# Experts with 4 KB weight rows, gate and up as three fp32r products, filled slots alone gathered and scattered to token rows

## The chip, the cores and the metric

The kernel runs on one core of a Trainium2 chip, as one program in one launch. The metric is the device time of the launch in microseconds (us), as the median over runs. A core has five instruction streams that wait for each other through semaphores: TensorE (PE, with its weight loads as PEld), VectorE (DVE), ScalarE (ACT), GpSimd (POOL) and SyncE (SP), which here only issues transfers. DMA engines, sixteen of them, move the data.

## The reference

One encoder layer is applied to 512 and to 1024 tokens with the same weights, 1536 tokens of 1024 features in all. Cut to what matters:

```python
h = h + parallel_mixer(rmsnorm(h, g_mix), ...)
h = h + memory_cross_attention(rmsnorm(h, g_xattn), rmsnorm(mem, g_mem), w_xq, w_xkv, w_xo)
h = h + hierarchical_moe(rmsnorm(h, g_moe), w_router_group, w_router_expert, w_exp_gate, w_exp_up, w_exp_down)
return rmsnorm(h, g_final)

def hierarchical_moe(hn, w_rg, w_re, w_gate, w_up, w_down):
    # top 1 of 4 groups, then the top 2 of its 8 experts; gates[n, e] is their weight, 0 for the other experts
    hg = jnp.einsum('nd,edf->nef', xf, w_gate)          # d 1024, f 128, e 32
    hu = jnp.einsum('nd,edf->nef', xf, w_up)
    act = jax.nn.silu(hg) * hu * gates[..., None]
    out = jnp.einsum('nef,efd->nd', act, w_down)
```

Everything is fp32. Each token has two experts, so 3072 pairs of token and expert have to be computed.

## The kernel before

The program is a list of stages: the mixer with its spatial gating and neighbourhood attention (to about 545 us of the trace), its output product, the memory cross-attention with the norm and logits of the router woven in (to 1043 us), the routing (to 1076 us), the experts (to 1343 us) and the last stage. Tokens are worked on in 12 tiles of 128 (`NT`).

Cross-attention and router. A list `stages`, written out at build time, fixes the order of TensorE's work; `order` is the same list with the norms' steps put between, and ScalarE and VectorE follow it. For the MoE norm, ScalarE squares a tile of `H`, GpSimd computes the reciprocal root (`rsqrt`, L670 to L675, two instructions on one column), VectorE multiplies (the `pre` step, L1206) into one of two buffers `hs`, SP stores that tile to `xn_moe` in HBM (L621), TensorE transposes it, and VectorE copies it out of PSUM times the column `g_moe` (`gain_evac`, L1167) for the logits. SP's queue holds, one behind the other, the loads of the cross-attention's weights, 24 stores of zeros to the result rows of the 24 possible overflow blocks (L614), the stores to `xn_moe`, with the weights of experts 0 and 3 behind the fourth, and the weights of six more experts once all logits are computed.

Routing. VectorE finds group and experts of each token; with TensorE's help every pair gets a slot in a table: 128 slots for each of the 32 experts, and `NOVER` = 24 overflow blocks for what exceeds 128. `slot_src` holds the token of every slot; empty slots hold token 0. `slot` holds the slot of every pair. How many overflow blocks are used is known only on the chip (`over_n`).

Experts. A block is 128 slots of one expert. GpSimd gathers its 128 rows of `xn_moe` with an indirect DMA (L760), two buffers `x_g`. TensorE transposes them, 8 times 128x128 (L1650), and VectorE copies them times `g_moe` to `x_gT` (L1167). With the weights as the stationary and `x_gT` as the moving operand TensorE computes gate and up, 16 fp32 matmuls of 128 columns (L1659); the trace shows each fp32 matmul as two, so 32. ScalarE takes the silu (L996), VectorE the product (L1370), which stands ready as `act_T`; TensorE makes the down product, 2 matmuls of 512 columns (L1666), after the transposes of the next block. ScalarE (L999) and VectorE (L1374) copy one half each to `y_st`, and ScalarE issues a plain store of the 128 rows to `y_exp` (L1002). Weights lie in 8 slots (`RING`); SP refills a slot when the down product of its block is done, by three loads of 512 KB: gate, up (L605, L606) and down (L607). Gate and up are read so that a partition gets 8 pieces of 512 bytes; down gives 4 KB a partition. The 32 blocks of the experts come first, partly in a loop (`expert_blocks`), then a loop over the possible overflow blocks with an `If` around each body.

Last stage. When all stores have landed, GpSimd gathers for each tile the two result rows of every token from `y_exp` (L779), four tiles ahead (`AHEAD`). VectorE adds each to `H` times its gate (L1388, two passes of 1024 columns), ScalarE squares (L1016), GpSimd takes the root, VectorE scales with `gf_row` (L1396), and SP stores. GpSimd issues the gathers of the tile four ahead before a tile's root.

The code uses elsewhere what the change brings to the experts: `split_products` (L418). A number is split in a rounded part, copied by ScalarE to fp32r (`make_hi`, L411), and the difference, by VectorE (`make_lo`, L416), and three fp32r products (L421 to L423) stand for one fp32 product.

## Time and profile before

| | |
|---|---|
| median of 3 runs | 1422.01 us (1419.4 to 1422.91) |
| the profiled execution | 1418.28 us, span 1416.6 us |
| busy: PE, PEld, DVE, ACT, POOL | 1212.8, 953.3, 575.6, 330.8, 193.2 us |
| DMA | 207.17 MB, mean 146 GB/s |
| routing starts (last logits done) | 1043.6 us |
| first gate and up product of the experts | 1084.2 us |
| last result copied out of PSUM | 1343.0 us |
| ScalarE: copy of 128x512 from PSUM (L999), silu of 128x128 (L996) | 597, 277 ns |
| VectorE: product of 128x128 (L1370), copy of 128x512 from PSUM (L1374) | 287, 692 ns |
| GpSimd: the two instructions of a root (L673, L675), median; an issued gather (L760), median | 190, 549, 936 ns |
| ScalarE: square of 128x1024 (L1016), and reading its sum | 1056, 186 ns |

The shares of busy time are averages over stages of very different kinds, so the page is read by stages. In the 40 slices of the page TensorE is near full up to slice 28, drops in the routing, and is empty in the last two slices; the DMA engines are full in the experts. In the rows below, a group of instructions stands with its line, engine, operation, shapes and count; `x` with a number is a count. The granted clock is a share of 2.4 GHz: 1.00 is 2.4 and 0.50 is 1.2 GHz.

### The profile page before, as it was taken

Reading aid. Unit: us, or ns where it says so; the run is one execution under the profiler, and the core shown is the slowest. Engines: PE = TensorE matmul, PEld = TensorE weight load, DVE = VectorE, ACT = ScalarE, POOL = GpSimd, SP = SyncE. Lnnn points to the kernel's source line nnn. Section 1 sums busy time; section 2 is a strip of 40 time slices with the busy share of each in tenths; the row PEclk is TensorE's granted clock in tenths of the full one; section 3 lists DMA queues with packets and bytes.
Section 4 is the critical chain, followed back from the end, with each engine's and each line's share of the span. In section 5 each row is a group of like instructions: output and inputs, shape, how many; then the busy total and the mean of one; then the engine's idle time right before and its main releaser. Section 6 shows DMA issues by size and latency. Waiting matters only on the chain.

```text
span 1416.6 us, 17949 instructions
## 1 busy us (share of the span) xinstructions
PE 1212.8 (86%) x6288; PEld 953.3 (67%) x6288; DVE 575.6 (41%) x1101; ACT 330.8 (23%) x719; POOL 193.2 (14%) x323
## 2 busy tenths in 40 slices
PE   3999999599998995999989989999955999988700
PEld 2888888488877884788844446667745888877600
DVE  4423222421126775333332155344374333333357
ACT  4322222400025553211110143223110111111112
POOL 0221111100012220000010000000001111111075
PEclk9999999899999997999989999999976999999955
DMA  7211111233166115433110930004166999999877
GB/s 232 70 53 59 59 59 30 66 78 73 30 147 176 25 26 178 153 89 89 44 60 0 312 104 0 15 15 134 60 201 194 369 368 370 368 363 358 288 279 254
DMA packets 180730, 207.17 MB, mean 146 GB/s; under 512 B 35775, under 2 KB 140223, under 8 KB 180671
## 3 DMA queue, kind: packets, MB, share of 16 engines
q1 hardware_dynamic: 160462, 139.81, 33.4%
q0 software_dynamic: 10944, 39.85, 7.9%
q10 hardware_dynamic: 9264, 26.74, 5.1%
q8 instruction: 34, 0.56, 0.2%
q14 instruction: 26, 0.21, 0.0%
HBM read 147.34 MB, written 55.10 MB: 143 GB/s over the span
## 4 chain that ended last, share of the span: by engine, by line
PE 65%; SPq 16%; DVE 6%; issue 4%; POOL 3%; DMA 3%; ACT 2%; ACTq 0%; POOLq 0%; DVEq 0%
PE bank L1605 13%; PE bank L421 12%; PE bank L423 12%; PE bank L422 12%; SPq L607 8%; SPq L606 5%; PE bank L1509 3%; PE bank L1489 3%; POOL at L779 2%; PE bank L1498 2%; DVE at L416 1%; PE bank L1444 1%; PE bank L1565 1%; PE bank L1659 1%; SPq L605 1%
## 5 line engine op out<-in xcount | busy, mean ns | idle before, releaser
L421 PE MATMUL bank<-at,at 128*128 128x512 f32 x768 | 310.8, 405 | 28.6 <-DVE at L416 18.7
L423 PE MATMUL bank<-at,at 128*128 128x512 f32 x768 | 303.4, 395 | 0.0
L422 PE MATMUL bank<-at,at 128*128 128x512 f32 x768 | 302.8, 394 | 0.0
L1605 PE MATMUL bank<-at,at 128*128 128x512 f32 (+1 forms) x560 | 186.0, 491 | 5.3 <-DVE at L1167 5.3
L421 PEld LDWEIGHTS bank<-at,at 128*128 128x128 f32 x768 | 147.1, 192 | 59.9 <-DVE at L416 20.3
L1659 PEld LDWEIGHTS bank<-at,at 128*128 128x128 f32 x1248 | 146.0, 194 | 36.7 <-issue 12.8
L423 PEld LDWEIGHTS bank<-at,at 128*128 128x128 f32 x768 | 146.4, 191 | 31.6
L422 PEld LDWEIGHTS bank<-at,at 128*128 128x128 f32 x768 | 147.3, 192 | 29.4
L1659 PE MATMUL bank<-at,at 128*128 128x128 f32 x1248 | 149.0, 279 | 13.4 <-DMA at<-in_w_exp_down 12.0
L1605 PEld LDWEIGHTS bank<-at,at 128*128 128x128 f32 x560 | 93.5, 195 | 90.3 <-issue 85.7
L416 DVE TENSOR_TENSOR at<-at,at 128x1024 fp32r<-128x1024 f32 (+2 forms) x42 | 78.9, 1885 | 138.5 <-ACT at L411 138.5
L673 POOL TENSOR_TENSOR at<-at 128x1 f32<-128x1 f32 x88 | 23.8, 271 | 702.2 <-ACT at L962 330.1
L1167 DVE TENSOR_TENSOR at<-bank,at 128x512 f32<-128x512 f32 x160 | 102.8, 684 | 29.4 <-PE bank L1650 28.4
L411 ACT ACTIVATE at<-at 128x1024 fp32r<-128x1024 f32 (+3 forms) x42 | 66.1, 1582 | 96.6 <-DMA at<-in_w_in 29.8
L1666 PE MATMUL bank<-at,at 128*128 128x512 f32 x156 | 73.4, 593 | 0.0
L760 POOL DMA_INDIRECT at<-xn_moe,at x40 | 37.6, 940 | 250.5 <-PE bank L1650 213.3
L892 ACT ACTIVATE at<-at,at 128x256 f32<-128x256 f32 (+1 forms) x96 | 51.7, 539 | 57.5 <-DVE at L1123 57.3
L1370 DVE TENSOR_TENSOR at<-at,bank 128x128 f32<-128x128 f32 x39 | 11.2, 287 | 130.4 <-PE bank L1659 130.4
L1239 DVE COPY at<-bank 128x512 f32<-128x512 f32 x20 | 13.8, 691 | 121.5 <-PE bank L1605 121.5
L1509 PE MATMUL bank<-at,at 128*128 (+1 forms) x448 | 58.2, 276 | 3.6 <-DMA at<-v_att 3.3
L999 ACT ACTIVATE at<-bank 128x512 f32<-128x512 f32 x39 | 23.3, 597 | 161.6 <-PE bank L1666 161.6
L1489 PE MATMUL bank<-at,at 128*128 (+2 forms) x192 | 57.0, 424 | 3.2 <-POOL at L727 3.2
(158 smaller groups left out, 1250.0 us busy)
## 6 DMA issues: line engine op xcount, KB each, us to landing
at<-in_w_exp_gate SPq DMA_DIRECT2D x39, 512.0 KB, 9.4
at<-in_w_exp_up SPq DMA_DIRECT2D x39, 512.0 KB, 11.1
at<-in_w_exp_down SPq DMA_DIRECT2D x39, 512.0 KB, 11.8
y_exp<-at ACTq DMA_DIRECT2D x39, 512.0 KB, 6.8
y_exp<-at SPq DMA_DIRECT2D x24, 512.0 KB, 7.5
at<-y_mix SPq DMA_DIRECT2D x12, 512.0 KB, 4.5
xn_moe<-at SPq DMA_DIRECT2D x12, 512.0 KB, 2.6
at<-in_w_in SPq DMA_DIRECT2D x2, 2048.0 KB, 12.3
```

Of the source, the lines that this page charges most:

```text
L416: nc.vector.tensor_tensor(lo, x, hi.bitcast(F32), ALU.subtract).then_inc(lo_made, 1)
L421: nc.tensor.matmul(out, w_hi, x_hi, start=(k == 0), stop=False)
L422: nc.tensor.matmul(out, w_lo, x_hi, start=False, stop=False)
L423: last = nc.tensor.matmul(out, w_hi, x_lo, start=False, stop=(k == len(terms) - 1))
L606: sp.dma_start(w_gu[n][:, 1], a["w_exp_up"][0, one].rearrange("e (k p) f -> p (e k) f", p=P)).then_inc(w_e_here[n], 16)
L607: sp.dma_start(w_dn[n], a["w_exp_down"][0, one].rearrange("e p d -> (e p) d")).then_inc(w_e_here[n], 16)
L1167: nc.vector.tensor_tensor(dst, bank[first_bank + n][:].rearrange("p (k t) -> p k t", k=4), g, ALU.mult).then_inc(done, 1)
L1489: nc.tensor.matmul(bank[2 * (s % 2) + n][:, 0:P * len(keys)], q, k, start=True, stop=True).then_inc(s_done, 1)
L1509: last = nc.tensor.matmul(bank[6 + s % 2][:, n * P:(n + 1) * P], na_pT[s % 2][:, n, k * P:(k + 1) * P], vals[:, 4 * kg + 2 * (s % 2) + n, ...
L1605: mm = nc.tensor.matmul(b if kind == "route" else b[:], w, x, start=(k == 0), stop=(k == len(steps) - 1))
L1659: mm = nc.tensor.matmul(out[:, 0:P], w_gu[n][:, half_gu, k], x_gT[n % 2][:, k], start=(k == 0), stop=(k == KT - 1))
L1666: mm = nc.tensor.matmul(bank[5 + k][:], act_T[n % 2], w_dn[n][:, k * HALF:(k + 1) * HALF], start=True, stop=True)
```

## The change

1. Gate and up weights are read so that a partition gets rows 8p to 8p+7 of a weight matrix, one piece of 4 KB. So k now counts rows within a partition, and `x` has to be in the same order: the MoE norm writes its features in that order (VectorE, with `g_moe` as a row `gm_row` multiplied in), so the gain is applied before the store and no longer when transposed tiles are copied. `gm_row` is loaded behind the last query product, at the place of a part of `h_T`, and no tile of the MoE norm is scaled before.
2. Empty slots get a token number that is out of bounds and are skipped by the gathers; the six gather buffers are cleared once, so that skipped rows hold finite numbers. Results are scattered by an indirect DMA of GpSimd to `y_tok`, row k x 1536 + token for the k-th expert of a token; `y_exp`, the zero fills and the issue by ScalarE go.
3. For the 32 experts gate and up are 24 fp32r products with x as the stationary operand and the 256 columns of gate and up as the moving one. x and weights are split by ScalarE and VectorE. The activations now come out with tokens on the partitions, so TensorE transposes them (one 128x128) and ScalarE copies them. Overflow blocks keep fp32 products, with x stationary too.
4. The down product of block b-1 stands behind gate and up of block b. There are 6 weight slots instead of 8; gate and up of a slot are refilled when its gate and up products are done, down when its down product is done. 6 gather buffers instead of 2. The blocks of the 32 experts are written out, with no loop.
5. Last stage: SP loads the two rows of each token from `y_tok` with plain loads, 6 tiles ahead. ScalarE multiplies the first with its gate, GpSimd adds `H`, VectorE adds the second times its gate.

The core of the diff:

```diff
-RING = 8
-AHEAD = 4
+RING = 6
+AHEAD = 6
@@ SP
-            sp.wait_ge(fill_made, 3)
-            for b in range(NE, NBLK):
-                sp.dma_start(y_exp[b * P:(b + 1) * P]..., zeros...).then_inc(unused_filled, 16)
+            sp.wait_ge(mm_done, n_groups["q", NCH - 1, XH - 1] + 1)
+            sp.dma_start(gm_row, a["g_moe"][0].partition_broadcast(P)).then_inc(consts_here, 16)
...
+                sp.dma_start(w_gu[n][:, 0], a["w_exp_gate"][0, one].rearrange("e (p k) f -> p (e k) f", p=P)).then_inc(w_e_here[n], 16)
...
+            for e in range(RING, NE):
+                sp.wait_ge(gu_done, e - RING + 1)
+                load_gate_up(e, e % RING)
+                sp.wait_ge(y_done, e - RING + 1)
+                load_down(e, e % RING)
...
+            sp.wait_ge(y_sent[0], 16 * (NE // 2) + 16 * ((used + 1) // 2))
+            sp.wait_ge(y_sent[1], 16 * (NE // 2) + 16 * (used // 2))
+                for k in range(2):
+                    sp.dma_start(y_g[t][k], y_tok[k * T + t * P:k * T + (t + 1) * P]).then_inc(yg_here[t % AHEAD], 16)
@@ GpSimd
+            for j in range(RING):
+                pool.memset(x_g[j], 0.0).then_inc(zeroed, 1)
...
+            for b in range(NE):
+                pool.wait_ge(xgt_done, 2 * (b + 1))
+                gather(b + RING)
+                scatter(b)      # waits for y_evac_s, y_evac_v of b
...
+            def add_first(t):
+                pool.wait_ge(f_gated, t + 1)
+                pool.tensor_tensor(y_g[t][0], y_g[t][0], H[:, t], ALU.add).then_inc(f_first, 1)
@@ ScalarE, a block
+                    split_xg(b + 1)
+                    split_expert(b + 1)
+                silu(b, b % 2)
+                if b >= 1:
+                    evac_y(b - 1, (b - 1) % 2, (b - 1) // 2)
+                evac_act(b, b % 2)
@@ ScalarE, last stage
+                nc.scalar.activation(y_g[t][0], y_g[t][0], ACT.Copy, scale=gate[:, 0, t:t + 1]).then_inc(f_gated, 1)
@@ VectorE
+                        dve.wait_ge(consts_here, 16 * 8)
+                        nc.vector.scalar_tensor_tensor(hs[n % 2]..., H[:, t]..., r, gm_row..., ALU.mult, ALU.mult).then_inc(n_ready, 1)
...
+                    split_xg(b + 1)
+                    split_expert(b + 1, 0)
+                gated(b, b % 2)
+                if b + 1 < NE:
+                    split_expert(b + 1, 1)
+                if b >= 1:
+                    evac_y(b - 1, (b - 1) % 2, (b - 1) // 2)
...
+                nc.vector.scalar_tensor_tensor(H[:, t], y_g[t][1], gate[:, 1, t:t + 1], y_g[t][0], ALU.mult, ALU.add).then_inc(f_add, 1)
@@ TensorE
+                split_products(bank[2 + j][:, 0:2 * FE].rearrange("p (h f) -> p h f", h=2),
+                               [(x_gT_hi[j][:, k], x_gT_lo[j][:, k], w_gu_hi[j][:, :, k], w_gu_lo[b % RING][:, :, k])
+                                for k in range(KT)]).then_inc(gu_done, 1)
...
+            for b in range(NE):
+                transpose_xg(b + 1, (b + 1) % RING, (b + 1) // RING)
+                gate_up(b)
+                if b >= 1:
+                    down(b - 1, (b - 1) % 2, (b - 1) % RING)
+                transpose_act(b, b % 2)
+            down(NE - 1, (NE - 1) % 2, (NE - 1) % RING)
+            def overflow(b, j, n, r, half):
+                gate_up_whole(b, j, n, r)
+                transpose_xg(b + 1, (n + 1) % RING, r + (n + 1) // RING)
+                transpose_act(b, j)
+                down(b, j, n)
```

## Rows read from the trace of the kernel before

**Rows 1.** Stretches: us, busy (count) PE, PEld, DVE, ACT, POOL; clock, DMA, GB/s.

```profile
1100.00:1250.00 150.00, 149.25 (x1069) 125.54 (x1068) 54.43 (x96) 21.26 (x49) 22.47 (x24) 1.00 1.08 368
...
1350.00:1380.00 30.00, 0.00 (x0) 0.00 (x0) 18.30 (x15) 5.86 (x11) 24.84 (x25) 0.50 0.90 314
```

**Rows 2.** DMA issues: tensors, queue, count, KB each, median us to landing.

```profile
at<-in_w_exp_gate SPq DMA_DIRECT2D x39, 512.0 KB, 9.4
...
at<-in_g_final SPq DMA_DIRECT2D x1, 512.0 KB, 4.0
```

**Rows 3.** The chain of waits from 1000 us: start us, us, what.

```profile
1080.89 1.96 PE bank L1650 x8
...
1084.21 5.93 PE bank L1659 x32
...
1098.89 3.57 PE bank L1659 x32
...
1102.47 0.87 PE bank L1650 x8
...
1103.34 1.73 PE bank L1666 x4
...
1203.08 4.44 SPq L607
...
1410.10 1.28 DVE at L1396
```

**Rows 4.** VectorE in order of time: start us, us, what [idle before].

```profile
1342.35 0.69 DVE L1374 COPY at<-bank 128x512 f32<-128x512 f32 x1 [0.54 <-PE bank L1666]
...
1357.18 2.60 DVE L1388 SCALAR_TENSOR_TENSOR at<-at,at,at 128x1024 f32<-128x1024 f32 x2 [14.15 <-DMA at<-y_exp,at]
...
1387.18 1.28 DVE L1396 SCALAR_TENSOR_TENSOR at<-at,at,at 128x1024 f32<-128x1024 f32 x1 [0.72 <-POOL at L675]
...
1391.70 1.29 DVE L1396 SCALAR_TENSOR_TENSOR at<-at,at,at 128x1024 f32<-128x1024 f32 x1 [0.72 <-POOL at L675]
```

**Rows 5.** Stretches inside w_xkv's load and inside loads of experts.

```profile
562.00:564.00 2.00, 0.00 (x0) 0.00 (x0) 1.97 (x3) 0.00 (x0) 0.00 (x0) 0.50 1.03 424
...
1062.00:1064.00 2.00, 0.00 (x0) 0.00 (x0) 1.79 (x7) 0.00 (x0) 0.00 (x0) 0.50 1.16 322
```

**Rows 6.** TensorE in order of time: fp32r of 512 and of 56 columns.

```profile
130.11 0.39 PE L423 MATMUL bank<-at,at 128*128 128x512 f32 x1
...
130.34 0.39 PE L421 MATMUL bank<-at,at 128*128 128x512 f32 x1
...
1073.12 2.76 PE L1640 MATMUL bank<-at,at 128*128 128x56 f32 x12 [2.70 <-DVE at L1352]
```

**Rows 7.** Groups by form, VectorE and ScalarE: xcount | busy us, mean ns | idle.

```profile
L1167 DVE TENSOR_TENSOR at<-bank,at 128x512 f32<-128x512 f32 x160 | 102.8, 684 | 29.4 <-PE bank L1650 28.4 <-PE bank L1565 0.8
...
L416 DVE TENSOR_TENSOR at<-at,at 128x1024 fp32r<-128x1024 f32 x32 | 39.2, 1225 | 111.3 <-ACT at L411 111.3
...
L1206 DVE TENSOR_SCALAR at<-at,at 128x1024 f32<-128x1024 f32 x28 | 20.8, 747 | 2.5 <-POOL at L675 2.5
...
L411 ACT ACTIVATE at<-at 128x1024 fp32r<-128x1024 f32 x24 | 25.2, 1052 | 48.5 <-DMA at<-in_w_in 24.6 <-DVE at L1034 12.9 <-DVE at L1167 11.0
```

**Rows 8.** The gathers of the experts (L760): from issue to landing.

```profile
DMA to landing us min/median/max: 4.2/7.2/8.8
```

**Rows 9.** VectorE and GpSimd at 270 us, in order of time.

```profile
269.72 4.13 DVE L1084 TENSOR_SCALAR at<-at,at 128x512 f32<-128x512 f32 x1 [1.68 <-POOL at L675]
...
269.64 3.94 POOL L709 MEMSET at<- 128x4608 f32 x1
```

**Rows 10.** GpSimd in the last stage, in order of time.

```profile
1397.64 1.48 POOL L675 TENSOR_TENSOR at<-at 128x1 f32<-128x1 f32 x1
```

**Rows 11.** Groups by form, GpSimd.

```profile
L727 POOL COPY at<-at 64x256 f32 x36 | 22.7, 631 | 73.0 <-PE bank L1489 71.8
...
L701 POOL TENSOR_SCALAR at<-at 128x1440 f32<-128x1440 f32 x1 | 1.7, 1691 | 0.1
```

359 lines of the change are left out of this document (215 added, 144 removed).

## Prediction

> **What bounds the kernel now.** Read the stretches view first: from 1100 to 1250 us TensorE is busy all but 0.75 us, and so are the DMA engines, at a share of 1.08 and 368 GB/s; from 1350 to 1380 us TensorE is idle, at the lower of its two granted levels (0.50, 1.2 GHz) [rows 1]. So two stages are at stake: the experts (39 blocks: 32, and 7 overflow blocks, by the count of issues [rows 2]) and the last stage. Then the chain of waits. Early in the experts it runs through TensorE alone, 3.57 us of gate and up, 0.87 us of transposes and 1.72 us of down products, 6.16 us a block; later through the sync queue, where an issue of one weight load lasts 4.44 us because the queue is backed up [rows 3]. A block moves three weight tensors of 0.52 MB [rows 2] and 128 rows of 4 KB each way, 2.62 MB, at 368 GB/s 7.1 us. That is over 6.16 us, so the 8 slots loaded ahead run out and the stage ends at the pace of the transfers: first gate-up at 1084.21 [rows 3], last copy of a result at 1342.35 plus 0.7 [rows 4]. In the last stage GpSimd paces: it issues two indirect gathers a tile, and final scalings of successive tiles stand 4.52 us apart (1387.18, 1391.70) [rows 4]. From 1343.05 to the span's end at 1416.6 are 73.55 us.
>
> **Bytes.** Weights stay 1.57 MB a block. Only the 3072 filled slots are now gathered and scattered, 12.6 MB each way, instead of 39 times 128 rows. The stage moves 61.3 + 25.2 = 86.5 MB instead of 102. What of the rate? A load in 4 KB rows ran at 424 GB/s, the expert loads alone, two thirds of them in 512 byte pieces, at 322 [rows 5]. All is 4 KB now; I take 400 to 420 GB/s in the mix (368, today's mix, is the low end). From block 0 to 31 some 50 MB of weights and 22 MB of rows move: 181 us at 400, 196 at 368. Six slots are full when the stage begins and a slot is refilled four blocks before its use, which covers some 13 us. 168 to 183 us is the demand of the transfers; TensorE will want 179 (below). So the transfers stop being the bound, narrowly.
>
> **TensorE per block.** Gate and up change from 32 half-products of 128 columns (3.57 us) to 24 fp32r products (hi·hi, lo·hi, hi·lo for 8 k) of 256 columns. No fp32r product of 256 columns is in the trace. An fp32r product of 512 columns starts 0.227 us after the one before, at the full clock (2.4 GHz); a 128 column half-product of fp32, which the chain gives 3.57/32 = 0.112 us, passes its columns twice, so it does as much array work; an fp32r product of 56 columns takes 2.76/12 = 0.23 us at the lower level, 0.115 at the full one [rows 3, 6]. Those set 0.112 to 0.120 (0.227 less half of the 0.213 that 512 columns take at 2.4 GHz); the far bound is 0.227, the price of 512. I take 0.116: 2.78 us. With transposes 0.87, down 1.72, and the new transpose of the activations 0.11, a block takes 5.48 us, 0.68 less than 6.16. The activations' round (silu, product, and now a transpose and a copy) lies behind the down products of the block before.
>
> **The other engines in a block.** ScalarE: two copies of x at 0.6, two of the weights at 1.05, silu 0.28, the turned activations 0.28, the result 0.6 (0.6 and 0.28 as in the table): 4.5 us. VectorE: two differences of x at 0.69, two of the weights at 1.23, the product 0.29, the result 0.69: 4.8 us [rows 7]. Both are under 5.48 and walked through in their order, each instruction after the one it waits for, no wait of TensorE ends later than its own work: the last difference for block b+1 ends about when the down products of b-1 do, the transposes of b+2 (0.87) ahead of its use. GpSimd now issues a gather and a scatter: 0.94 us each when undisturbed, as in the table. A result buffer is wanted again 2 x 5.48 - 0.7 = 10.3 us after it is full; the scatter takes about 1.2 us to get its descriptors past a VectorE instruction and lands 7.2 us after, as the gathers do [rows 8]. 8.4 against 10.3 us. For what slips in these two narrow places I add 0.1: 5.6 us a block.
>
> **Overflow blocks.** They stay fp32: 16 half-products of 256 columns at 0.215 (half of 1.73/4 [rows 3]) are 3.44 us; their activations' round isn't hidden: 0.9 for silu and product, 0.11, then 0.6 for the copy of x that ScalarE does first, 0.3, 1.72 for down. 6.75 us each, 47 for seven.
>
> **When the stage ends.** The transposes of block 0 began at 1080.89 at the lower level and took 1.96 us; block 0's half-products took 5.93 instead of 3.57, so the level rose among them [rows 3]. One more VectorE step ahead of the table makes the start 1081.2; transposes 2.0, the split 1.5, block 1's transposes 2.0, and 24 products at 2.8 plus the same 2.0 or so for the level: 1091.5. The second block waits for its split weights: 1096.4. 30 x 5.6 gives 1264.4, its rest 4.2, overflow 47.3, last copy 0.9, branches 1.5: 1318.3, without what comes ahead.
>
> **Ahead of the experts.** The gain of the MoE norm moves to a row that is loaded when the last query product is done; a like row landed in 4.0 us [rows 2]. VectorE waits for it in line, with the result of the first output product queued behind it; TensorE has two banks, 3.4 us of products, before it waits as well: +3.1 (0 if later waits absorb it). The norm's product goes from 0.75 [rows 7] to 1.28 us (a pass of that kind [rows 4]); three of them stand in the tail: +1.6. The six clearings of gather buffers on GpSimd (0.9 us each by 3.94 us for 4608 columns [rows 9]) run while VectorE routes: 0 to 5, I take 1. Table step 0.3. Sum +6 (bounds 0 to 11). The 24 zero fills were hidden behind products: 0. So the last copy is at 1324.3, 18.7 us earlier.
>
> **The last stage.** Loads can start when the last scatter has landed: 1.0 to issue, some 4.2 in all (the quickest gather [rows 8]), then the first two loads of a queue of twelve, 4.7: 9.0 after the last copy (the gathers: 14.1, to 1357.18 [rows 4]). Bytes: 1.57 MB a tile, 3.8 us at 410 GB/s. But the work of a tile moves: ScalarE scales (1.06) and squares (1.25), GpSimd adds two 128x1024 tiles, VectorE does two three-operand passes instead of three. GpSimd and VectorE shut each other out: a VectorE product over 512 columns took 4.13 us beside a 3.94 us GpSimd clearing, where 1024 columns take 0.75, and the second instruction of GpSimd's root took 1.48 us instead of 0.55 beside a VectorE pass [rows 9, 10]. If a long GpSimd addition and a VectorE pass with two tile operands do so too, the tile costs their sum. The addition isn't in the trace: a one-operand pass over 1440 elements takes 1.69 us, 1.20 for 1024; a copy of 256 takes 0.63, 2.5 for 1024 [rows 11]. With two operands I take twice the first, 2.3. Sum: 2.3 + 0.19 + 0.55 (the root, as in the table) + 2 x 1.28 = 5.6 us a tile, against 4.52. First sum of rows ready at 9.0 + 1.06 + 2.3 = 12.4; 11 x 5.6 = 61.6; last pass, square, root, scaling 4.7; last store 5.2 (from 1411.4 [rows 3] to 1416.6). 83.9 us against 73.55: +10.3.
>
> The Trainium skill, SBUF — State Buffer, section "SBUF: two separate sides", states that the port pair is held for a whole instruction by either a GpSimd instruction or a VectorE one in a two-port mode, or one with two SBUF inputs when GpSimd reads SBUF. The rows show the first kind and GpSimd's side of the second; that a long GpSimd addition stops VectorE no row shows. By this rule the last stage goes as in my sum; without it as in the first rival. The GPSIMD Engine Reference, section "Performance versus the Vector engine", gives 4497 ns for an addition of 2048 fp32; half of that, an estimate, is 2.25 us and would leave the sum as it is.
>
> **Sum.** -18.7 + 10.3 = -8.4: span 1408.2. The profiled execution took 1418.28, 1.7 over its span; the median of the runs is 1422.01, 3.7 above it. 1422.0 - 8.4 = 1413.6; I say 1413. Its own range, from 1.2 or 2.5 us for the addition, 5.4 to 5.9 us a block and 0 to 11 us ahead: 1399 to 1428.
>
> **Rivals.** (1) The last stage overlaps. GpSimd then needs 3.0 us a tile, VectorE 2.6, and bytes set 3.8: 12.4 + 41.8 + 4.7 + 5.2 = 64.1, 9.5 less than now; with the experts 28.2 less: 1394. For it: two VectorE passes took 2.60 us, as ever, beside GpSimd's issues of gathers [rows 4]. Against: the 4.13 us row. Chance 0.24. (2) Slower: the scatter or the transfers pace the blocks. VectorE's weight differences shut GpSimd out, the scatter lands over 10.3 us after its buffer is full, and the copy of b+2 waits; at 6.3 us a block it costs 0.7 x 32 = 22: 1436. It decides when a landing exceeds some 9 us (8.4 expected); slower than before from 5.9 us a block on. Chance 0.17. (3) The change doesn't do what it says: an fp32r product of 256 columns costs 0.227. Then 24 x 0.111 x 32 = 85 us more, 1498. Against: 128 and 512 columns of fp32 go as their columns. Chance 0.06.
>
> **How the numbers follow.** Forecast 0.53, rivals 0.24, 0.17, 0.06. 0.3% is 4 us, about what a measurement of this kernel tells from no change: 1418 and 1426 are the borders. Of the forecast's 0.53, 0.31 lies under 1418 and 0.11 within; with the first rival faster is 0.55, same 0.12, slower 0.33. 8 in 10 takes in the first rival and most of the second: 1388 to 1438.
>
> **What will show it.** Starts of successive fp32r products 0.116 us apart in a block; blocks 5.5 to 5.7 us apart with TensorE idle for nothing; DMA near 400 GB/s with short sync issues; overflow blocks 6.7 apart; VectorE passes of 1.28 us stretched to 3.5 beside GpSimd additions of 2.3 in the last stage, tiles 5.6 apart. A last stage with tiles under 4.5 us apart, or blocks over 6, makes the prediction wrong.

## The result, and the profile after

The median of the changed kernel is 1427.34 us (1422.74 to 1430.34, 15 runs), that of the kernel before, run beside it, 1421.02 us (1414.3 to 1423.38, 15 runs). The ratio is 1.0042, 95% interval 1.003 to 1.0055: slower, by 6 us, where 1413 and "faster" were forecast. The profiled execution has a span of 1425.7 us, 9.1 above the one before; the profile of before is of an execution that was 2.7 us quicker than its median (1418.28 against 1421.02), that of after is the median itself, so the difference of the spans is some 3 us too large.

Where it went is read by laying four points of time beside each other. All are read from the two traces: the last copy of router logits, the first silu of an expert block, the silu of block 31 (the last of the 32 experts), and the end of the last copy of a result.

| | before | after | difference |
|---|---|---|---|
| last logits copied (start) | 1043.6 | 1062.7 | +19.1 |
| first silu, block 0 | 1088.03 | 1110.86 | +22.8 |
| block 0 to block 31 | 198.6 | 182.4 | -16.2 |
| block 31 to the last copy's end (7 overflow blocks) | 56.4 | 54.3 | -2.1 |
| last copy's end to the end of the span | 73.6 | 78.2 | +4.6 |
| sum of the last four | | | +9.1 |

The experts are shorter, as the change wanted. What is lost is lost ahead of them and behind them.

Ahead of them. The norm's pass by its line after (duration min/median/max in ns, first and last start; the second line is what it waited for, us and times); the pass of before is in [rows 7]:

```profile
L1278 DVE SCALAR_TENSOR_TENSOR at<-at,at,at x12: 2053/2140/2362, 938.9 to 1051.0; 128x1024 f32<-128x1024 f32 x12
...
  DMA at<-in_g_moe: 3.0, 1
```

The new pass takes 2.14 us in the median, against 0.75. The one wait for the gain row is 3.0 us. In the same stretch GpSimd's root of the norm is stretched beside it, and TensorE runs dry (stretches of after; columns as in [rows 1]):

```profile
L687 POOL TENSOR_TENSOR at<-at x10: 189/700/1508, 953.8 to 1049.9; 128x1 f32<-128x1 f32 x10
```

```profile
980.00:990.00 10.00, 6.54 (x39) 5.65 (x38) 4.84 (x7) 3.12 (x6) 1.15 (x2) 0.85 0.80 319
...
1020.00:1030.00 10.00, 6.83 (x39) 5.76 (x38) 4.05 (x5) 1.15 (x2) 1.12 (x2) 0.90 0.14 54
...
1050.00:1060.00 10.00, 9.80 (x53) 9.59 (x53) 5.93 (x9) 0.00 (x0) 3.42 (x14) 0.59 0.26 105
```

TensorE is busy 6.5 and 6.8 us of 10, and the granted clock falls to 0.85, 0.90 and, in the last products of the router, 0.59. Dips of the clock are in the kernel before as well (0.68 from 1010 to 1020 us); what is new is the tail. Here are the 10 us ahead of the last copy of logits, before and after:

```profile
1033.60:1043.60 10.00, 9.60 (x82) 8.90 (x81) 5.78 (x12) 1.15 (x2) 2.49 (x13) 1.00 0.27 107
```

```profile
1052.70:1062.70 10.00, 9.94 (x48) 9.80 (x47) 3.25 (x8) 0.00 (x0) 0.87 (x3) 0.50 0.13 52
```

TensorE is busy in both, at 2.4 GHz before and at 1.2 GHz, the lower of the two levels, after: the tail of the stage is paid at half speed.

In the experts, TensorE in order of time, and then ScalarE's silus of blocks 14 to 16, both after:

```profile
1204.22 0.28 PE L421 MATMUL bank<-at,at 128*128 128x256 f32 x1
1204.34 0.28 PE L422 MATMUL bank<-at,at 128*128 128x256 f32 x1
1204.45 0.28 PE L420 MATMUL bank<-at,at 128*128 128x256 f32 x1
```

```profile
1188.27 0.28 ACT L1039 ACTIVATE at<-bank 128x128 f32<-128x128 f32 x1
1195.20 0.26 ACT L1039 ACTIVATE at<-bank 128x128 f32<-128x128 f32 x1
1202.20 0.26 ACT L1039 ACTIVATE at<-bank 128x128 f32<-128x128 f32 x1
```

An fp32r product of 256 columns starts 0.12 us after the one before (median 0.120; the 24 of a block stand 0.123 apart in the mean). The first 14 gaps between silus are 5.53 us in the mean; those shown, at block 14, are 6.93 and 7.00, and from block 14 to 28 the mean is 6.35. So there are two halves: TensorE paces the first, something else the second. The wait that is named there is ScalarE's, for a load (us in total, times, longest, from 1180 to 1280 us):

```profile
ACT at L410 <- DMA at<-in_w_exp_down: 25.2, 15, 2.5
```

The last stage, VectorE and GpSimd in order of time, one tile:

```profile
1385.50 2.35 POOL L806 TENSOR_TENSOR at<-at,at 128x1024 f32<-128x1024 f32 x1
1385.57 3.37 DVE L1502 SCALAR_TENSOR_TENSOR at<-at,at,at 128x1024 f32<-128x1024 f32 x1 [0.44 <-POOL at L689]
...
1387.82 1.17 POOL L687 TENSOR_TENSOR at<-at 128x1 f32<-128x1 f32 x1
1388.86 1.27 DVE L1494 SCALAR_TENSOR_TENSOR at<-at,at,at 128x1024 f32<-128x1024 f32 x1
1389.06 1.48 POOL L689 TENSOR_TENSOR at<-at 128x1 f32<-128x1 f32 x1
...
1390.57 3.36 DVE L1502 SCALAR_TENSOR_TENSOR at<-at,at,at 128x1024 f32<-128x1024 f32 x1 [0.44 <-POOL at L689]
```

VectorE's final pass is issued 0.07 us after GpSimd's addition of 2.35 us and lasts 3.37 instead of 1.28 [rows 4]: it does its work when the addition has ended. The root's small instructions (1.17, 1.48) last as long as the VectorE passes beside them. Tiles stand 5.00 us apart, against 4.52 [rows 4].

### The profile page after: what moved, and what is told of

Read it like the earlier page. It is cut to its first block, busy times and chain, and to the rows that moved or that the text cites. A ratio compares the mean times of both kernels' runs of the same rounds, so it can differ in the third digit from the quotient of the medians.

```text
span 1425.7 us, 17488 instructions
## 1 busy us (share of the span) xinstructions
PE 1212.4 (85%) x5959; PEld 939.1 (66%) x5959; DVE 664.7 (47%) x1146; ACT 449.6 (32%) x905; POOL 277.5 (19%) x362
## 3 DMA queue, kind: packets, MB, share of 16 engines
q0 software_dynamic: 13824, 31.48, 6.0%
## 4 chain that ended last, share of the span: by engine, by line
PE 74%; DVE 7%; DMA 6%; issue 4%; POOL 3%; ACT 3%; SPq 2%; ACTq 0%; POOLq 0%; DVEq 0%
PE bank L420 14%; PE bank L422 13%; PE bank L421 13%; PE bank L1711 13%; PE bank L1791 3%; PE bank L1615 3%; DMA at<-in_w_exp_down 3%; PE bank L1595 3%; DVE at L415 2%; PE bank L1777 2%; PE bank L1604 2%; PE bank L1757 2%; POOL at L806 1%; PE bank L1550 1%; ACT at L410 1%
## 5 line engine op out<-in xcount | busy, mean ns | idle before, releaser
L420 PE MATMUL bank<-at,at 128*128 128x512 f32 (+1 forms) x1024 | 387.9, 379 | 27.8 <-DVE at L415 17.9
L421 PE MATMUL bank<-at,at 128*128 128x512 f32 (+1 forms) x1024 | 377.4, 369 | 0.0
L422 PE MATMUL bank<-at,at 128*128 128x512 f32 (+1 forms) x1024 | 377.2, 368 | 0.0
L420 PEld LDWEIGHTS bank<-at,at 128*128 128x128 f32 x1024 | 197.4, 193 | 61.7 <-DVE at L415 21.8
L415 DVE TENSOR_TENSOR at<-at,at 128x1024 fp32r<-128x1024 f32 (+2 forms) x106 | 157.0, 1484 | 168.3 <-ACT at L410 155.3
L422 PEld LDWEIGHTS bank<-at,at 128*128 128x128 f32 x1024 | 197.2, 193 | 32.2
L421 PEld LDWEIGHTS bank<-at,at 128*128 128x128 f32 x1024 | 197.6, 193 | 29.5
L1711 PE MATMUL bank<-at,at 128*128 128x512 f32 (+1 forms) x560 | 192.2, 503 | 11.1 <-DVE at L1295 5.8
L687 POOL TENSOR_TENSOR at<-at 128x1 f32<-128x1 f32 x88 | 37.2, 423 | 702.7 <-ACT at L986 336.6
L410 ACT ACTIVATE at<-at 128x1024 fp32r<-128x1024 f32 (+3 forms) x106 | 130.5, 1268 | 119.6 <-DMA at<-in_w_in 29.8
L1711 PEld LDWEIGHTS bank<-at,at 128*128 128x128 f32 x560 | 97.2, 204 | 99.3 <-issue 92.4
L1791 PE MATMUL bank<-at,at 128*128 128x512 f32 x156 | 74.2, 597 | 3.3 <-ACT at L1043 3.3
L1316 DVE COPY at<-bank 128x512 f32<-128x512 f32 x20 | 13.8, 691 | 122.7 <-PE bank L1711 122.7
L986 ACT ACTIVATE at<-at 128x1024 f32<-128x1024 f32 x28 | 29.6, 1056 | 120.0 <-PE bank L1671 112.2
L785 POOL DMA_INDIRECT y_tok<-at,at x39 | 39.9, 1024 | 140.9 <-DVE at L1463 92.1
L778 POOL DMA_INDIRECT at<-xn_moe,at x45 | 58.6, 1301 | 41.9 <-issue 41.2
L689 POOL TENSOR_TENSOR at<-at 128x1 f32<-128x1 f32 x88 | 57.7, 656 | 6.9
L1615 PEld LDWEIGHTS bank<-at,at 128*128 128x128 f32 x448 | 54.6, 194 | 3.3 <-issue 2.9
L1757 PE MATMUL bank<-at,at 128*128 128x128 f32 x320 | 43.3, 280 | 7.5 <-issue 6.0
```

Source lines behind the costliest of these rows:

```text
L410: nc.scalar.activation(hi, x, ACT.Copy).then_inc(hi_made, 1)
L415: nc.vector.tensor_tensor(lo, x, hi.bitcast(F32), ALU.subtract).then_inc(lo_made, 1)
L420: nc.tensor.matmul(out, w_hi, x_hi, start=(k == 0), stop=False)
L421: nc.tensor.matmul(out, w_lo, x_hi, start=False, stop=False)
L422: last = nc.tensor.matmul(out, w_hi, x_lo, start=False, stop=(k == len(terms) - 1))
L689: pool.tensor_tensor(rs[:, col:col + 1], ms_eps[:, col:col + 1], neg_half, ALU.pow).then_inc(out_sem, 1)
```

## The experiments

The theory after the result: the permuted VectorE pass (its two tile operands are read in steps of 32 bytes, its result is written straight) costs what is lost ahead of the experts; in the second half of the experts the weights come too slowly; in the last stage the GpSimd addition shuts VectorE out. Rivals: the norm's later place and the wait for its row; TensorE or the scatter in the experts; the transfers in the last stage.

### The gain row alone, in the kernel before

```diff
+            sp.wait_ge(mm_done, n_groups["q", NCH - 1, XH - 1] + 1)
+            sp.dma_start(gm_row, a["g_moe"][0].partition_broadcast(P)).then_inc(gm_here, 16)
             sp.wait_ge(fill_made, 3)
             for b in range(NE, NBLK):
...
-                    nc.vector.tensor_scalar(hs[n % 2], src, rs[:, 4 + n % 2:5 + n % 2], None, ALU.mult).then_inc(n_ready, 1)
+                        nc.vector.scalar_tensor_tensor(hs[n % 2], H[:, t], r, gm_row, ALU.mult, ALU.mult).then_inc(n_ready, 1)
```

> The kernel before with one part of the change alone: the gain of the MoE norm is loaded as a row once the last query product is done, the norm's VectorE pass becomes a product of three operands with that row, all in straight order, and it may not stand ahead of that point; the evacuations of the transposes drop the gain. Theory (the permuted pass is what costs ahead of the experts): the pass takes 1.28 us instead of 0.75, and the last logits, at 1043.6 before, come 3 to 7 us later, the time is 0.2 to 0.5% above before. Rival (the later place and the wait for the row cost it, whatever the order of the elements): the logits come 15 to 19 us later and the time is 1.0 to 1.4% above before.

1453.04 us (1449.54 to 1454.03, 4 runs), 1.0222 of before (1.0189 to 1.0256); last logits at 1079.2, 35.6 us late. By its numbers neither theory. Its trace from 940 to 1060 us shows what it was (DMA issues there, and what was waited for from 950 us):

```profile
y_exp<-at SPq DMA_DIRECT2D x24, 512.0 KB, 6.9
```

```profile
ACT at L966 <- DMA xn_moe<-at: 25.6, 1, 25.6
```

The 24 zero fills, 12.6 MB, which the kernel before issues from 783 us on and has behind it by then, were held back by the new wait on the sync queue and ran ahead of the stores of the normed rows; ScalarE waited 25.6 us for one such store, whose buffer it wanted. The fault is the experiment's place for the wait, not the row. It is also a lesson on this change: its early wait on SP is cheap only since the fills are gone.

### The same, in permuted order

```diff
-                        nc.vector.scalar_tensor_tensor(hs[n % 2], H[:, t], r, gm_row, ALU.mult, ALU.mult).then_inc(n_ready, 1)
+                        nc.vector.scalar_tensor_tensor(hs[n % 2].rearrange("p (k q) -> p k q", k=KT), H[:, t].rearrange("p (q k) -> p k q", k=KT), r,
+                                                       gm_row.rearrange("p (q k) -> p k q", k=KT), ALU.mult, ALU.mult).then_inc(n_ready, 1)
...
-                sp.dma_start(w_gu[n][:, 0], a["w_exp_gate"][0, one].rearrange("e (k p) f -> p (e k) f", p=P)).then_inc(w_e_here[n], 16)
+                sp.dma_start(w_gu[n][:, 0], a["w_exp_gate"][0, one].rearrange("e (p k) f -> p (e k) f", p=P)).then_inc(w_e_here[n], 16)
```

> The kernel before with the gain row as above, and the pass reads and writes in the permuted order (32 byte steps), with the router and the expert gate and up weights in 4 KB pieces to match; fp32 products, gathers, scatters and the last stage are as before. Theory (the permuted pass costs): each pass 2.1 to 2.4 us, last logits 15 to 19 us after 1043.6. Rival (place): the same as the kernel with the straight row, under 2 us apart. For the experts: if 512 byte pieces held the transfers back (322 GB/s against 424), the stage from the first gate and up to the last copy (258.8 us before) becomes 5 to 13 us shorter, since TensorE at 6.16 us a block bounds it then; if they did not, it stays within 3 us.

1443.9 us (1443.07 to 1447.21, 4 runs), 1.017 (1.0136 to 1.0204). The same fills stand in its way, so its front (logits at 1086.3) says little: 7 us over the straight one. The pass takes 2055/2150/2354 ns; it reads in steps and writes straight, other than the expectation has it. What the run does show: from the first result copy's start to the last 234.3 us, against 249.6 before. The pair is repeated below with the fills out of the way.

### The straight norm in the changed kernel

```diff
-                        nc.vector.scalar_tensor_tensor(hs[n % 2].rearrange("p (k q) -> p k q", k=KT), H[:, t].rearrange("p (q k) -> p k q", k=KT), r,
-                                                       gm_row.rearrange("p (q k) -> p k q", k=KT), ALU.mult, ALU.mult).then_inc(n_ready, 1)
+                        nc.vector.scalar_tensor_tensor(hs[n % 2], H[:, t], r, gm_row, ALU.mult, ALU.mult).then_inc(n_ready, 1)
...
-                    mm = nc.tensor.transpose(bank[k // 4][:, (k % 4) * P:(k % 4 + 1) * P], x_g[n][:, k * P:(k + 1) * P], ident)
+                    mm = nc.tensor.transpose(bank[k // 4][:, (k % 4) * P:(k % 4 + 1) * P], x_g[n].rearrange("p (q k) -> p k q", k=KT)[:, k], ident)
```

The router's weights are loaded in the order that suits.

> The changed kernel with the norm's pass in straight order; the router's weights are loaded to suit, and the expert transposes read the gathered rows in steps of 8 elements, so that the 4 KB weight pieces stay. Theory: the pass takes 1.28 us, the last logits come at 1047 to 1052 instead of 1062.7, all behind it moves by as much, and the time falls by 10 to 15 us, to 0.994 to 0.998 of before. Rival (place and wait): logits at 1060 or later, the time within 3 us of the changed kernel, 1.003 of before. If TensorE's strided reads cost, the transposes of an expert block take over 0.87 us and the blocks stand over 5.7 us apart instead of 5.58.

1415.11 us (1412.0 to 1418.55, 10 runs), 0.996 (0.9943 to 0.9977); the changed kernel has 1.0042. One pass in another order turns slower into faster, by 12 us of the medians. By line:

```profile
L1278 DVE SCALAR_TENSOR_TENSOR at<-at,at,at x12: 1274/1278/1285, 938.8 to 1042.2; 128x1024 f32<-128x1024 f32 x12
...
  DMA at<-in_g_moe: 3.1, 1
  POOL at L689: 0.4, 1
```

```profile
L1311 DVE COPY at<-bank x12: 186/196/196, 956.1 to 1048.8; 128x36 f32<-128x36 f32 x12
```

The last logits come at 1048.8: 13.9 us earlier than with the permuted pass, and 5.2 after the kernel before. The wait for the row is still there (3.1 us), as is the later place; they are not the cause. The twelve passes are 10.7 us shorter together (15.3 against 26.1 us of busy time). The rest hangs on them, and the delay can be followed along the stage: the copies of logits come later in the changed kernel by 3.1 us at the first tile, 2.5 at the third, 5.9 at the fourth, 8.5 at the ninth, and 13.9 at the twelfth. GpSimd's root has a median of 0.191 us again. From 980 to 1050 us the clock is much the same (0.94 here, 0.93 in the changed kernel); in the 10 us ahead of the last copy it is 0.98 here and 0.50 there.

How sure are these differences? Single executions reach this stage up to 4 us apart: eight kernels here that share the straight norm and the same front have their last logits between 1047.5 and 1051.7. Counted from the last norm pass ahead of the MoE norm (at 884.7 us before, 885.8 in the changed kernel) the scatter is gone: 163.0 to 163.3 us to the last logits in all eight and in the kernel before with the straight row behind the fills (below), 176.9 and 176.7 in the two permuted ones, 158.9 before. So the order costs 13.7 us, and row, place and wait together some 4.2.

The step of 32 bytes is now in TensorE's reading of the gathered rows:

```profile
L1756 PEld LDWEIGHTS bank<-at,at x320: 185/193/226, 1087.2 to 1330.2; 128*128 128x128 f32 x160
L1756 PE MATMUL bank<-at,at x320: 272/274/450, 1087.2 to 1330.3; 128*128 128x128 f32 x160
```

The same in the changed kernel, with straight reads:

```profile
L1757 PEld LDWEIGHTS bank<-at,at x320: 137/140/231, 1100.9 to 1343.6; 128*128 128x128 f32 x160
L1757 PE MATMUL bank<-at,at x320: 272/273/448, 1101.0 to 1343.7; 128*128 128x128 f32 x160
```

The gathered rows are what the weight loads of the transposes read, and these take 193 ns instead of 140. They run beside the matmuls of 274 ns, so almost nothing of it is seen in the time: the blocks of the first half stand 5.59 us apart instead of 5.57, and the means of the two halves are those of the changed kernel (5.54 and 6.36 us).

### 512 byte pieces in the changed kernel

The norm straight, and gate and up loaded with "e (k p) f", so that the transposes read straight too.

> The changed kernel with the norm's pass in straight order and the gate and up weights in 512 byte pieces again, so that nothing reads in steps. Up to the experts it does what the kernel above does. If the 4 KB pieces are needed (322 to 368 GB/s with 512 byte pieces), a block of about 2.25 MB takes 6.1 to 7.0 us, the blocks after the slots loaded ahead stand over 6 us apart, and the experts take 12 to 40 us longer than in the kernel above. If the smaller number of bytes alone is enough, the blocks stand 5.6 us apart and both kernels agree within 3 us.

1429.96 us (1425.59 to 1432.86, 8 runs), 1.0066 (1.0045 to 1.0086). Block 0 to 31 takes 194.6 us against 182.7 with 4 KB pieces, +11.9, just under the low end of the first expectation; the medians of the time are 14.9 apart. The first 11 gaps are 5.6 or less, against 14, so what is loaded ahead lasts three blocks less; from block 14 to 28 the mean is 6.87 against 6.36. Stretches from 1180 to 1280 us, first with 512 byte pieces, then with 4 KB (the last two columns are DMA share, which is the mean busy share of the DMA engines, and GB/s):

```profile
1180.00:1280.00 100.00, 88.49 (x551) 68.41 (x550) 64.34 (x89) 59.40 (x104) 29.65 (x29) 0.98 1.04 332
```

```profile
1180.00:1280.00 100.00, 93.46 (x595) 73.57 (x595) 69.98 (x95) 63.51 (x112) 36.47 (x33) 1.00 0.98 365
```

### The last stage's additions on VectorE

```diff
-                pool.wait_ge(f_gated, t + 1)
-                pool.tensor_tensor(y_g[t][0], y_g[t][0], H[:, t], ALU.add).then_inc(f_first, 1)
...
-                nc.vector.scalar_tensor_tensor(H[:, t], y_g[t][1], gate[:, 1, t:t + 1], y_g[t][0], ALU.mult, ALU.add).then_inc(f_add, 1)
+                nc.vector.scalar_tensor_tensor(H[:, t], y_g[t][0], gate[:, 0, t:t + 1], H[:, t], ALU.mult, ALU.add).then_inc(f_first, 1)
+                nc.vector.scalar_tensor_tensor(H[:, t], y_g[t][1], gate[:, 1, t:t + 1], H[:, t], ALU.mult, ALU.add).then_inc(f_add, 1)
```

The norm is straight, and ScalarE's multiplications by the first gate go as well.

> The changed kernel with the norm's pass in straight order, and in the last stage the additions go back to VectorE: three passes a tile in its own order, as before, with the plain loads kept; GpSimd only does the root, ScalarE only the squares. Theory (a GpSimd addition and VectorE's passes shut each other out, so the tile costs their sum, 5.01 us): the tile takes 3 passes of 1.28 us, 3.85 to 4.0 us, and no pass is stretched; from the last result copy to the end 62 to 65 us instead of 78.8; the time is 14 to 16 us below the kernel that differs in the straight norm alone, 1399 to 1401 us. Rival (the transfers of 1.57 MB a tile set it, at the 367 GB/s of the experts): tiles 4.3 us apart, 67 to 69 us from the last copy, 1404 to 1406. If neither the engines nor the transfers but a chain of waits across engines set it, the tile stays near 5 us.

1398.35 us (1397.8 to 1402.84, 5 runs), 0.984 (0.9824 to 0.9856): it beats both kernels. VectorE in the last stage:

```profile
1383.11 1.28 DVE L1494 SCALAR_TENSOR_TENSOR at<-at,at,at 128x1024 f32<-128x1024 f32 x1 [0.44 <-POOL at L689]
...
1384.31 1.28 DVE L1484 SCALAR_TENSOR_TENSOR at<-at,at,at 128x1024 f32<-128x1024 f32 x1
1385.62 1.28 DVE L1486 SCALAR_TENSOR_TENSOR at<-at,at,at 128x1024 f32<-128x1024 f32 x1
1386.83 1.28 DVE L1494 SCALAR_TENSOR_TENSOR at<-at,at,at 128x1024 f32<-128x1024 f32 x1
```

No pass is stretched; the final passes go from 1351.29 to 1393.1, 3.80 us a tile; from the end of the last copy (1336.77) to the end 64.4 us, against 78.85 in the kernel that differs in this alone (1412.9 less 1334.05). The transfers move 402 GB/s from 1345 to 1365 us and 379 from 1365 to 1385, so they are near, but do not set the pace: after the first tile VectorE waits for no load, only for GpSimd's root, 3.4 us in all.

### fp32 products for all blocks

With the straight norm; blocks 0 to 31 use the overflow blocks' gate and up product, and nothing is split:

```diff
-                gate_up(b)
+                gate_up_whole(b, b % 2, b % RING, b // RING)
```

> The changed kernel with the straight norm, and gate and up of all blocks as fp32 products (16 half-products of 256 columns, x stationary) as in the overflow blocks; no splits of weights or rows on ScalarE and VectorE. Theory (in the second half of the experts the transfers pace, 6.2 us a block, and TensorE's gain counts only in the first half at 5.58): the block takes 3.44 + 0.87 + 1.72 + 0.11 = 6.14 us throughout, the experts become 4 to 8 us longer than in the kernel with split products, the time 1419 to 1423. Rival (the transfers are slowed by what ScalarE and VectorE do, or TensorE paces throughout): the same time within 2 us, or 18 us longer (32 x 0.57).

1422.27 us (1418.52 to 1424.12, 10 runs), 1.0007 (0.9993 to 1.0021). The gaps are 6.16 us from the second to the last; block 0 to 31 takes 190.3 us, 7.6 more than with split products. The first 14 gaps are 0.57 longer, the later ones 0.19 shorter. TensorE's 0.6 us a block is worth 7 us, not 19 (32 x 0.6), since in the second half it had been spent waiting. The transfers that hold the split blocks at 6.36 us in the second half do not hold these: at 6.16 from the start, what is loaded ahead is used up so slowly (0.2 us a block) that it lasts for all 32.

### Empty slots gathered too

Two runs on the straight norm: an empty slot reads the last token's row, or, in the second, the row of its own number.

```diff
-            nc.vector.scalar_tensor_tensor(slot_src, bank[2][:, 0:NBLK], float(2 * T), second, ALU.add, ALU.subtract).then_inc(table_ready, 1)
+            step(nc.vector.scalar_tensor_tensor(second, bank[2][:, 0:NBLK], float(2 * T), second, ALU.add, ALU.subtract))
+            nc.vector.tensor_scalar(slot_src, second, float(T - 1), None, ALU.min).then_inc(table_ready, 1)
```

> The changed kernel with the straight norm, and the gathers read a row for every slot, empty ones too (the last token's row), while the scatters still leave them out: 128 rows a gather instead of some 79. Theory (the second half of the experts goes at the transfers' pace, 360 to 380 GB/s): 0.2 MB more a block, so blocks of 6.7 to 6.8 us instead of 6.2 there and the pace is reached earlier: 10 to 17 us longer, 1425 to 1432 us. Rival (the landing of the scatter paces, or TensorE): within 3 us of the kernel that differs in the norm alone, 1415.

1416.94 us (1414.69 to 1419.99, 9 runs), 0.997 (0.9957 to 0.9984): 1.8 us more than without those rows (the intervals overlap), where bytes at a fixed rate gave 10 to 17.

```diff
+            step(nc.vector.tensor_scalar(over_f8, second, float(T), token[1][:, 0:1], ALU.is_ge, ALU.mult))
+            nc.vector.tensor_tensor(slot_src, over_f8, second, ALU.add).then_inc(table_ready, 1)
```

> As the kernel whose gathers read a row for every slot, but an empty slot reads the row of its own number (128 different rows) and not one row over and over. Theory A (leaving empty slots out saves bytes and little time; the weights' own arrival paces): as with the one row, 1415 to 1419 us, experts 0 to 3 us longer than without the empty rows. Theory B (in that run the one row was read cheaply, and bytes count): 6.7 to 6.8 us a block in the second half, 1425 to 1432 us.

1416.58 us (1415.87 to 1417.66, 5 runs), 0.9966 (0.9953 to 0.9979). Block 0 to 31: 184.8 us with different rows, 184.7 with the one row, 182.7 without. So it is not that one row is read cheaply. Here is the same stretch as above, with the spread rows:

```profile
1180.00:1280.00 100.00, 91.04 (x582) 71.79 (x582) 69.38 (x94) 62.26 (x110) 33.49 (x32) 1.00 1.01 394
```

394 GB/s against 365, at nearly the same pace of blocks. The rate is no constant of the stage: with fewer gathered bytes in it, it falls. Leaving the empty slots out of the gathers saves 11 MB (178.9 moved against 189.9) and 2 us. GpSimd's queue has 13824 packets with and without them (42.5 and 31.5 MB): a row that is left out gives up its bytes, not its packet.

### Fewer weight bytes

With the straight norm; from block 6 on the down load of the main blocks fetches 64 of 1024 columns, and the other 960 are weights of an earlier expert, so this kernel's results are not the layer's.

```diff
-                load_down(e, e % RING)
+                sp.dma_start(w_dn[e % RING][:, 0:64], a["w_exp_down"][0, e, :, 0:64]).then_inc(w_e_here[e % RING], 16)
```

> The changed kernel with the straight norm, and from block 6 on only the first 64 of the 1024 columns of the down weights are loaded (that part of the down products then works on older weights), at the same place and with the same waits: 1.08 MB of weights a block instead of 1.57. Theory (the arrival of weight bytes paces the second half of the experts): every one of the 31 gaps between blocks is 5.6 us, the experts become 10 to 12 us shorter than in the kernel with the straight norm alone, 1403 to 1405 us. Rival (the order of release and landing, whatever the bytes: a load is issued so late that its latency shows): gaps over 6 us stay, under 4 us shorter.

1405.77 us (1402.68 to 1408.42, 4 runs), 0.9895 (0.9879 to 0.9911); block 0 to 31 172.6 us, 10.1 less. Silus at the place where the changed kernel's gaps had grown:

```profile
1173.70 0.28 ACT L1039 ACTIVATE at<-bank 128x128 f32<-128x128 f32 x1 [0.23 <-PE bank L422]
1179.28 0.28 ACT L1039 ACTIVATE at<-bank 128x128 f32<-128x128 f32 x1 [0.23 <-PE bank L422]
1184.87 0.28 ACT L1039 ACTIVATE at<-bank 128x128 f32<-128x128 f32 x1 [0.23 <-PE bank L422]
```

5.59 us apart, as are all but the first. So it is the arrival of the weights: scatters, gathers and the order of the waits are unchanged in this run. 12.8 MB of weights less give 10 us, where 11 MB of gathered rows less gave 2.

### The down weights waited for by their own product

Additions on VectorE and the straight norm, and:

```diff
-                act.wait_ge(w_e_here[e % RING], 48 * (e // RING + 1))
+                act.wait_ge(w_e_here[e % RING], 32 * (e // RING + 1))
...
+            def down(b, j, n, r):
+                pe.wait_ge(w_d_here[n], (32 if n == 5 else 16) + 16 * (r + 1))
```

> The kernel with the straight norm and VectorE's additions in the last stage, and one wait more exact: the down weights count on semaphores of their own, ScalarE's split of a block waits for its gate and up weights alone and the down product waits for the down weights. In the second half of the experts ScalarE had stood 20 to 25 us for the down load. Theory (that stretch is paced by how fast weights arrive over all, so a load that is waited for later only moves the wait): experts 1 to 4 us shorter at most, time 1394 to 1398 us. Rival (the late release of the down slot and the wait of the wrong operation pace it): blocks back at 5.6 us throughout, experts 9 to 11 us shorter, 1387 to 1390 us.

1399.33 us (1398.95 to 1400.48, 5 runs), 0.9843 (0.9829 to 0.9856): no gain on 1398.35. Block 0 to 31 takes 181.1 us instead of 182.5. The wait has moved to the load before it, as a stage paced by arrival would have it:

```profile
ACT at L411 <- DMA at<-in_w_exp_up: 22.0, 14, 2.4
```

### The gain row in the kernel before, behind the fills

The first two kernels again, with SP's wait and the row's load behind the 24 zero fills.

> The kernel before with the gain row alone, in straight order, as in the earlier run of that kind, but the row's load and its wait stand behind the 24 zero fills of the sync queue instead of ahead of them. Theory (in the earlier run the fills, 12.6 MB, had been held back by the new wait into the stretch from 950 to 1050 us and stood ahead of the stores of the normed rows, and that was the 35 us): logits 4 to 7 us after 1043.6 as with the straight norm in the changed kernel (1048.8), time 1424 to 1429. Rival (a three-operand pass and its place cost more in the kernel before than in the changed one): logits past 1060.

1423.21 us (1421.01 to 1424.7, 10 runs), 1.0018 (1.0004 to 1.0032); the last logits at 1049.7, 6.1 after the kernel before (4.1 by the count from the norm pass above). Row, wait and place together cost 2 us in the time. Of the 35.6 us by which the first of these kernels had its logits late, 29.5 were the fills.

> The kernel before with the gain row behind the zero fills, its pass in permuted order, and the router, gate and up weights in 4 KB pieces; nothing else is changed. Theory: against the same kernel in straight order (logits done at 1049.9, experts 249.3 us from the first to the last result copy, 1423.2 us) the logits come 12 to 15 us later, by the longer pass, and the experts are 13 to 16 us shorter, by the 4 KB pieces, with TensorE at 6.16 us a block: time 1421 to 1426. Rival (the 4 KB pieces helped in the earlier run of this kind only because its stage began later): experts 245 us or more, time 1432 or more.

1422.8 us (1420.05 to 1425.14, 10 runs), 1.0012 (1.0001 to 1.0023). The two kernels take the same time and have two differences that cancel. The last logits copy of each, then their last result copies:

```profile
L1246 DVE COPY at<-bank x12: 183/196/196, 957.0 to 1049.7; 128x36 f32<-128x36 f32 x12
...
L1385 DVE COPY at<-bank x39: 690/692/693, 1098.4 to 1347.7; 128x512 f32<-128x512 f32 x39
```

```profile
L1247 DVE COPY at<-bank x12: 189/196/196, 958.8 to 1062.2; 128x36 f32<-128x36 f32 x12
...
L1386 DVE COPY at<-bank x39: 691/692/694, 1111.9 to 1346.3; 128x512 f32<-128x512 f32 x39
```

The permuted pass costs 12.5 us ahead of the experts (1062.2 less 1049.7), the 4 KB pieces give 14.9 in them (249.3 to 234.4), half in the 32 experts and half in the 7 overflow blocks. With them the blocks stand 6.16 us apart to the last and TensorE is not kept waiting, at 2.62 MB a block:

```profile
1180.00:1280.00 100.00, 100.00 (x719) 84.45 (x718) 36.72 (x65) 14.31 (x33) 14.98 (x16) 1.00 0.97 391
```

These are two sides of one idea, the new order of k: it was bought on VectorE at nearly its whole worth.

## Why the prediction was wrong, point by point

The sum missed the profiled span by 17.5 us (1425.7 against 1408.2). Three terms make it up: 13.8 ahead of the experts, 9.4 in them, -5.7 in the last stage.

**Ahead of the experts: the norm's pass was mis-sized, and this alone turned the sign (the kernel with the straight pass is faster than before).** Predicted +6, with 1.28 us a pass, of which three counted; block 0's transposes were to start at 1087.2. They started at 1100.95. With the straight pass they start at 1087.2, on the forecast, and the wait for the row is 3.1 us as forecast. Executions differ by some us there, so the exact hit is luck; but 4.2 us up to the logits where 3.1 and 1.6 were added, and 1.2 from there to the transposes where 1.3 was, say that place, wait, clearings and table step were sized well (the table step's 0.3 us stands twice in the sum, in 1081.2 and in +6). What failed is the step that took 1.28 "a pass of that kind" [rows 4] for a pass whose operands are read in steps of 8 elements. It takes 2.14. No row showed such a pass; a bound upward was called for and none was given: even with the top of the range, 11 us, the transposes would have begun at 1092.2, nearly 9 us too early. It failed a second time in counting: only the three passes of the tail were priced, while of the 13.9 us by which the straight pass is quicker, 8.5 are there by the ninth of twelve tiles. And the drop of TensorE's clock in the tail was in no term.

The Trainium skill, SBUF — State Buffer, section "Door 1: The DMA port swizzle", states that SBUF has 16 byte lines and that a step is free up to 4 fp32 elements. Here the step is 8, and the pass takes 2.14 against 1.28 us: the trace agrees for VectorE, and this was the rule that spoke against the change. TensorE's weight loads with the same step take 193 against 140 ns, so the trace agrees there too, only that next to nothing of it is seen in the time.

**TensorE's block: right.** 0.120 us a product, 0.116 forecast and 0.120 the upper of the near bounds; 5.57 us a block where nothing else holds it, 5.6 forecast; overflow blocks 6.99 against 6.75 (the terms listed for them add up to 7.07, not 6.75). That rules out the third rival (0.227).

**The transfers: the step "the transfers stop being the bound, narrowly" failed.** It divided bytes by a rate of 400 to 420 GB/s. 392 GB/s came from 1130 to 1180 us, while the slots were being used up, and 367 from 1180 to 1280 us, the low end that was named and not chosen; by that low end the prediction's own demand was 183 us, over TensorE's 179, and 182.4 were measured from block 0 to 31. The mean gap of the 31 is 5.88. The run with fewer weight bytes has 172.6 us where the same kernel with all of them has 182.7: that is the term. What was wrong in it is the step from bytes left out to time won. With the empty rows gathered as well the same stretch has 394 GB/s, near the rate that was taken, and the stage is 2 us longer; with them left out the rate falls to 365. The second rival had the right mechanism in half of the stage: the transfers paced it, at 6.35 us a block for 14 blocks instead of 6.3 for 32. Its other half, the scatter, is not seen: ScalarE and VectorE waited 5.6 and 5.4 us in all for a landing, over the whole stage. Why the rate falls stays open. What a left-out row costs in a queue was not measured by itself, and neither were the six slots instead of eight nor the scatters in place of plain stores, though the kernel before with 4 KB pieces moves 391 GB/s from 1180 to 1280 us.

**The parts of the experts' gain.** 4 KB pieces 12 (in the changed kernel) to 15 us (in the one before, overflow blocks included), split products 7.6, empty rows not gathered 2. They share one bound, so they don't add to a sum of their own. The prediction gave most of it to TensorE.

**The last stage: the mechanism right, the size too large.** Addition 2.35 us (2.3 forecast), first VectorE pass 12.4 us after the last copy (12.4), VectorE shut out beside the addition: all as in the text. The tile is 5.00 instead of 5.6, since the root's instructions, priced at 0.74 in a row of their own, wait out VectorE's passes and so lie mostly beside them. +4.6 instead of +10.3. The first rival (overlap, 64.1 us) didn't come. That the version with VectorE's additions takes 64.4 us is no support for it: there three VectorE passes of 1.28 us make the tile, where the rival had the bytes' 3.8.

The Trainium skill, SBUF — State Buffer, section "SBUF: two separate sides", states that one of the two, a GpSimd instruction or a VectorE one with two SBUF inputs when GpSimd reads SBUF, has the shared port pair for a whole instruction. The trace agrees: the pass of 1.28 us lasts 3.37 with the addition ahead of it, and 1.28 again with the addition gone.

**The range.** The time, 1427, lies in 1388 to 1438, and just inside the forecast's own 1399 to 1428 (whose three bounds added up give 1388 to some 1430). That is luck in good part: two terms were off by 13.8 and 9.4 us, each beyond or near its bound, and the third, off by -5.7, took a quarter of it back.

## What to carry to other kernels

A layout that makes a transfer quicker is paid for where the layout is made: ask which engine writes the new order, and whether one that reads it (here the weight loads of TensorE's transposes, longer but hidden) could take the step instead of one that is in line, and price a stepped pass upward from the row of a straight one, for every pass that has a waiter. Work moved from VectorE to GpSimd is not off VectorE's path while both read whole tiles from SBUF: 14 us of this kernel's last stage came back when it was moved back. Bytes left out are not time won until a run shows that the rate holds. A stage that is close to its transfers has no fixed rate: bound it by the lowest rate that its trace shows, and look at how long what is loaded ahead lasts.

## What the runs showed of the hardware

A VectorE pass that multiplies a 128x1024 fp32 tile by a column and by a second tile takes 1.28 us straight and 2.05 to 2.36 us with its two tiles read in steps of 32 bytes (whether the first or the second read costs it is open). TensorE's fp32 weight loads of 128x128 with the same step take 193 ns against 140, beside matmuls of 274. fp32r products of 256 columns start 0.120 us apart at 2.4 GHz. A GpSimd addition of two 128x1024 fp32 tiles takes 2.35 us. Weight loads in 512 byte pieces ran at 332 GB/s where 4 KB pieces ran at 365, in the same stage. The Trainium skill, DMA: Bandwidth & Descriptors, section "Specifications", gives 512 bytes as enough for line rate; here the measurement differs, by 12 us of the experts, and decides. An indirect gather that skips rows by a token number out of bounds keeps its count of packets. The overflow blocks stand 6.08 us apart in the kernel before with 4 KB pieces and 6.99 in the changed one, whose activations' round is not hidden there, as the forecast had it.
